# VectorE's order within an attention step: the scan in front of the low half of the turned tile

## The reference

```python
z = einsum('bqhd,bkhd->bhqk', qb, k) * (SB_HEAD_DIM ** -0.5)
log_beta = log_sigmoid(z)
log_1m = where(mask, log_beta - z, 0.0)
after = cumsum(log_1m, axis=3, reverse=True) - log_1m
a = where(mask, exp(log_beta + after), 0.0)
out = einsum('bhqk,bkhd->bqhd', a, v)
```

## Time and profile before

| what | value |
|---|---|
| median of 3 runs | 2603.29 us (2601.96 to 2605.12) |
| the profiled execution's own time | 2601.78 us |
| its span in the profile | 2600.0 us |
| granted TensorE clock, mean | 0.995 |
| TensorE busy | 2519.7 us, 97% |
| VectorE busy | 1576.0 us, 61% |
| ScalarE busy | 1152.9 us, 44% |
| POOL busy | 1169.5 us, 45% |

### The profile page before, as it was taken

One profiled execution on the slowest core, in us unless ns is written; L12 is line 12 of the kernel. 1 busy time (PEld: TensorE's weight loads), 2 busy tenths in 40 slices (PEclk: granted clock), 3 DMA queues, 4 the chain that ended last, 5 costly groups with the idle time before them and its releaser, 6 DMA issues.

```text
span 2600.0 us, 37523 instructions
## 1 busy us (share of the span) xinstructions
PE 2519.7 (97%) x13864; PEld 2149.3 (83%) x13864; DVE 1576.0 (61%) x2125; ACT 1152.9 (44%) x1932; POOL 1169.5 (45%) x1028
## 2 busy tenths in 40 slices
PE   8999899999999999999999999999999999999998
PEld 8978798787878888878788887878878887889997
DVE  3266236676435357787744477887775355867766
ACT  4366326665233135566531265656654213343333
POOL 3465435755223135456631174556653214344444
PEclk9999999999999999999999999999999999999999
DMA  6597956764446233443254244333533512233222
GB/s 229 182 277 249 343 178 190 220 207 137 136 135 244 82 114 95 132 121 112 89 188 157 97 121 119 102 110 110 148 96 114 200 65 94 75 100 110 94 95 86
DMA packets 211014, 373.91 MB, mean 144 GB/s; under 512 B 30768, under 2 KB 105136, under 8 KB 208784
## 3 DMA queue, kind: packets, MB, share of 16 engines
q1 hardware_dynamic: 210832, 371.50, 45.4%
HBM read 303.34 MB, written 68.09 MB: 143 GB/s over the span
## 4 chain that ended last, share of the span: by engine, by line
PE 83%; DVE 6%; issue 4%; DMA 2%; ACT 2%; POOL 2%; SPq 1%; POOLq 0%; ACTq 0%; DVEq 0%
PE bank L1278 27%; PE bank L1340 19%; PE bank L1228 8%; PE bank L1187 7%; PE bank L1286 7%; PE bank L1087 5%; PE bank L1134 4%; PE bank L1103 4%; DVE left L1901 1%; DMA gw_lo_raw<-in_w_in_dram 1%; POOL gw_lo L2545 1%; POOL later_lad L2571 1%; PE bank L1210 1%; DMA v_st<-v_cache_scratch 0%; DMA mixT<-mixT_scratch 0%
## 5 line engine op out<-in xcount | busy, mean ns | idle before, releaser
L1278 PE MATMUL bank<-x1T,gw_hi 128*128 128x512 f32 (+1 forms) x2336 | 712.5, 388 | 4.9 <-DVE hT_lo_raw L2002 3.5
L2475 POOL TENSOR_TENSOR beta<-beta,left 128x512 f32<-128x512 f32 (+2 forms) x326 | 350.3, 1075 | 348.6 <-DVE left L1901 347.9
L1278 PEld LDWEIGHTS bank<-x1T,gw_hi 128*128 128x128 f32 x2336 | 419.2, 189 | 84.6 <-issue 4.6
L1278 PE MATMUL bank<-x1T,gw_lo 128*128 128x512 f32 (+1 forms) x1168 | 448.1, 384 | 0.0
L2502 POOL TENSOR_TENSOR gw_lo<-gw_lo_raw,gw_hi 128x1024 fp32r<-128x1024 f32 x70 | 181.8, 2597 | 423.8 <-ACT gw_hi L1529 423.6
L1228 PE MATMUL bank<-x1T,gw_hi 128*128 128x256 f32 (+2 forms) x1472 | 356.9, 335 | 13.1 <-DVE x1T L2264 8.9
L1452 ACT ACTIVATE aT<-bank 128x512 fp32r<-128x512 f32 (+2 forms) x326 | 173.6, 533 | 424.9 <-PE bank L1103 377.3
L2177 DVE TENSOR_TENSOR acc<-bank,acc 128x512 f32<-128x512 f32 x312 | 213.7, 687 | 211.3 <-PE bank L1340 208.0
L1886 DVE TENSOR_TENSOR aT<-bank,aT 128x512 fp32r<-128x512 f32 (+2 forms) x326 | 197.2, 605 | 196.5 <-ACT aT L1452 195.2
L1340 PE MATMUL bank<-dw_hi,hT_hi 128*128 128x512 f32 x728 | 295.2, 405 | 10.8 <-issue 8.4
L1340 PE MATMUL bank<-dw_lo,hT_hi 128*128 128x512 f32 x728 | 286.7, 394 | 0.0
(11 more groups left out here) (220 smaller groups left out, 4709.2 us busy)
## 6 DMA issues: line engine op xcount, KB each, us to landing
gw_lo_raw<-in_w_gate_dram SPq DMA_DIRECT2D x88, 512.0 KB, 3.7
gw_lo_raw<-in_w_up_dram SPq DMA_DIRECT2D x88, 512.0 KB, 3.8
dw_lo_raw<-in_w_down_dram SPq DMA_DIRECT2D x86, 512.0 KB, 4.4
gw_lo_raw<-in_w_in_dram SPq DMA_DIRECT2D x64, 512.0 KB, 4.7
k_st<-kT_scratch SPq DMA_DIRECT2D x160, 128.0 KB, 4.1
v_st<-v_scratch SPq DMA_DIRECT2D x80, 256.0 KB, 4.3
q_st<-qT_scratch SPq DMA_DIRECT2D x128, 128.0 KB, 4.0
wo_raw<-in_w_out_dram SPq DMA_DIRECT2D x16, 1024.0 KB, 5.6
```

Source lines behind the costliest of these rows:

```text
L1278: m = pe.matmul(gu_bank(g, n)[:, 0:w], gw[L % 4][a][:, k, :], x1T[x][:, k, first:first + w], start=k == 0 and s == 0, stop=k == KD - 1 and ...
L2475: pool.tensor_tensor(x[:, 0:w], x[:, 0:w], left[n % RL][:, 1:w + 1], ALU.mult).then_inc(a_done, 1)
```

## The change

On VectorE, within `attention`, the block that takes the low half of the turned tile (item s - 7) moves from in front of the block that scans (item s - 1) to behind it. Waits, operands and tiles are the same, and no other engine's program is touched.

```diff
--- before.py
+++ after.py
@@ -1879,12 +1879,6 @@
                         dve.wait_ge(o_stored[og % 2], 32 * (og // 2))
                     dve.wait_ge(o_low, og + 1)
                     dve.tensor_tensor(o_t[rows, :], bank[O_BANK][0:HD, :], o_part[:, :], ALU.add).then_inc(o_sum, 1)
-                u = lo + s - AT_HI
-                if lo <= u < hi:
-                    cols = columns(u)
-                    dve.wait_ge(aT_hi, u + 1)
-                    dve.tensor_tensor(aT[u % 2][1][:, cols], bank[t_at[u]][:, cols], r32(aT[u % 2][0][:, cols]),
-                                      ALU.subtract).then_inc(aT_lo, 1)
                 n = lo + s - AT_LEFT
                 if lo <= n < hi:
                     w, out = ITEMS[n].width, left[n % RL]
@@ -1900,6 +1894,12 @@
                         added = begin[:, BW - w:BW][:, ::-1]
                     dve.tensor_tensor_scan(out[:, 0:w][:, ::-1], bank[z_at[n]][:, 0:w][:, ::-1], added, out[:, w:w + 1],
                                            ALU.mult, ALU.add).then_inc(left_done, 1)
+                u = lo + s - AT_HI
+                if lo <= u < hi:
+                    cols = columns(u)
+                    dve.wait_ge(aT_hi, u + 1)
+                    dve.tensor_tensor(aT[u % 2][1][:, cols], bank[t_at[u]][:, cols], r32(aT[u % 2][0][:, cols]),
+                                      ALU.subtract).then_inc(aT_lo, 1)
                 u = lo + s - AT_V - 2
                 if lo <= u < hi and closes_group(u) and not ITEMS[u].sample:
                     og = ITEMS[u].group
```

## The result

The changed kernel takes 2778.51 us (median, 2773.11 to 2782.61) against 2603.23 us for the kernel before: 1.0675 times as long, with a 95% interval of 1.0662 to 1.0687. The profiled execution took 2776.15 us, 174.4 us more than the one of before; its span is 2774.3 us. The forecast was 2804 us in a range of 2725 to 2868.

A forecast was written before the change was run, and what follows sets the result against it. TensorE was taken to bound the kernel. Summed turning shortfalls of 210 us, less 9 us of scan waits, plus 0, gave 201 us on 2601.78 us: 2803 us, 2804 as median; range 2725 to 2868 us.

The forecast's parts named there:

- The loop's length: Turning, copy, sigmoids, scan, low half, next turning through bank 6: at least 4.28 us, against TensorE's own 2.76 us.
- near ticks: Attention ticks one slot after the tick before: 106 of 119 predicted short, by 132 us in all.
- far ticks: Attention ticks two or more slots after the last: 133 of 177 two-slot ticks short by 78 us; the loop alone gives 43.
- so the shortfalls add: TensorE's stalls before turnings are never made up, so the ticks' shortfalls sum: 210 us, or 175 if VectorE's work gets ahead.
- the subtraction: Per tick, on the trace before: low half's new end plus hand-over, less next turning's start; positive shortfalls total 210 us.
- Waits for the scan: TensorE never again meets an unfinished scan at the scores: 9 us given back, at most 27.0.
- VectorE's tick ends later: Low half no longer fills VectorE's wait for the sigmoids, delaying work behind it: nothing taken, bound 29 us.
- TensorE's idle: Sign in the profile after: grows by some 200 us, all ahead of the last attention step.
- The slack that covers it: Rival: room between low half and next turning hides the move, within 0.2%, 2603 us; chance 0.03.
- the gain: Rival: where VectorE comes late the scan ends 0.6 us sooner; 9 to 27 us given back, 2577 to 2594 us; chance 0.02.
- The partial payment at 105 us: Rival: only short ticks cost, 132 us less 27 of waits: 2707 us, up to 2735; chance 0.11.
- The clock rival: Rival: stalls also lower TensorE's granted clock, ten to twenty drops, 27 to 54 us: 2830 to 2857 us; chance 0.06.

The follow-up runs named there:

- experiment 1: Kernel before, swap made only in ticks one slot after the previous tick: 2716.5 us; only in ticks two or more slots after: 2667.0 us.
- the one with the doubled low half: Changed kernel with the low half's subtraction done a second time into its own tile, in front of the one that counts: 2939.5 us, 161.0 above the changed kernel.

## Why the prediction was right, point by point

**What bounds, and how little the list of waits said.** Right. TensorE waited 5.6 us for the low half before, and yet moving it by 1.2 to 2.2 us cost 175 us. A wait of zero had 0.8 us behind it.

**The loop's length.** Right: forecast 4.28 us, 4.29 in the rows above. From copy to copy, the median of the 119 near ticks went from 2.85 to 4.28 us, and of the 177 ticks two slots apart from 4.05 to 4.29.

**The sum over the ticks.** The forecast was 132 us for the near and 78 us for the far ticks, and 43 for the far ones if VectorE's late work doesn't count. With the start of each next turning taken from both traces and the growth of their distance added up tick by tick, the near ticks lost 127 us and the far ones 50, together 178. (The expectations of experiment 1 count from copy to copy, which gives 105 and 73, the same total.) So the near term was right, and **the mis-sized term is the 78 us of the far ticks: 50 of them were paid.** The step that failed is "so the shortfalls add": they were read from the trace of before, one tick at a time, and a stall in a tick ahead gives the other engines time, which makes the next shortfall smaller. The far ticks fall into three groups:

| far ticks (two slots) | ticks | forecast | paid in the change | paid when only far ticks are swapped |
|---|---|---|---|---|
| VectorE late by the add of a down product | 43 | 25 us | 24 us | 25 us |
| VectorE late by other work | 22 | 18 us | 8 us | 15 us |
| VectorE's lateness adds nothing | 112 | 35 us | 19 us | 33 us |

The prediction took only VectorE's late work (35 us) for something that might shrink. But the down adds, 19 of these 35 us, wait for TensorE's own product and move with it, as in the far step shown above; they were paid. Of the 28 us that are missing, 16 are in the ticks of the third group, where the prediction saw no doubt: there ScalarE had been late. In those of them that the forecast had short, its second sigmoid came sooner behind the turning by 16 us in all, and by 2 us when only the far ticks are swapped. That the total of 50 lies so near the 43 of the lower end is luck. One tick of the third group, before:

```profile
1207.92 0.60 PE L1103 MATMUL bank<-begin,beta 128*128 128x128 f32 x4
1208.47 1.15 ACT L1496 ACTIVATE acc<-acc,rstd 128x1024 f32<-128x1024 f32 x1
...
1209.51 0.59 ACT L1452 ACTIVATE aT<-bank 128x512 fp32r<-128x512 f32 x1
...
1211.86 0.60 PE L1103 MATMUL bank<-begin,beta 128*128 128x128 f32 x4
```

After:

```profile
1283.89 1.15 ACT L1496 ACTIVATE acc<-acc,rstd 128x1024 f32<-128x1024 f32 x1
...
1285.08 0.63 PE L1103 MATMUL bank<-begin,beta 128*128 128x128 f32 x4 [1.58 <-DVE aT L1901]
...
1285.74 0.60 ACT L1452 ACTIVATE aT<-bank 128x512 fp32r<-128x512 f32 x1 [0.71 <-PE bank L1103]
...
1289.37 0.63 PE L1103 MATMUL bank<-begin,beta 128*128 128x128 f32 x4 [0.16 <-DVE aT L1901]
```

Before, a norm's scaling on ScalarE (line 1496) held the copy back to 1.59 us behind the turning, and the subtraction put the next turning 1.28 us late. After, the same scaling fell into the stall of 1.58 us ahead of the turning, the copy came after 0.66 us, and the step grew from 3.94 to 4.29 us only. With the far ticks alone swapped there is no such stall ahead: the same step took 5.21 us, 1.27 more than before.

One tick of the second group, before:

```profile
1110.20 0.38 PE L1103 MATMUL bank<-begin,beta 128*128 128x128 f32 x2
...
1111.91 0.60 ACT L1462 ACTIVATE bank<-bank 128x512 f32<-128x512 f32 x1
...
1112.36 1.59 DVE L2163 TENSOR_TENSOR hT_lo<-hT_lo_raw,hT_hi 128x512 fp32r<-128x512 f32 x1
1113.87 0.41 DVE L1886 TENSOR_TENSOR aT<-bank,aT 128x256 fp32r<-128x256 f32 x1
...
1114.52 0.27 PE L1103 MATMUL bank<-begin,beta 128*128 128x128 f32 x1
```

After:

```profile
1170.03 0.41 PE L1103 MATMUL bank<-begin,beta 128*128 128x128 f32 x2 [1.56 <-DVE aT L1901]
...
1171.61 0.68 DVE L2163 TENSOR_TENSOR hT_lo<-hT_lo_raw,hT_hi 128x512 fp32r<-128x512 f32 x1
1171.76 0.60 ACT L1462 ACTIVATE bank<-bank 128x512 f32<-128x512 f32 x1
1172.40 1.28 DVE L1895 TENSOR_TENSOR_SCAN left<-bank,left,zero_t 128x512 f32<-128x512 f32 x1
1173.60 0.40 DVE L1901 TENSOR_TENSOR aT<-bank,aT 128x256 fp32r<-128x256 f32 x1
...
1174.36 0.27 PE L1103 MATMUL bank<-begin,beta 128*128 128x128 f32 x1
```

Before, VectorE was at the hidden tile's low half until 1113.95, 2.04 us after that second sigmoid began, and the subtraction put the turning 1.09 us late. After, the same piece was done at 1172.29, ahead of the sigmoid's end, 1.51 us better: 0.60 us because it started sooner (the turning ahead had stalled for 1.56 us), and 0.91 us because it was shorter itself (see the last section). The turning came after 4.33 us, 4.32 before. Where no near tick makes such stalls, in the run that swaps only the far ticks, these ticks lost 74 us from turning to turning, near the 78 of the subtraction, while the near ticks, not swapped there, got 7 us shorter.

**Waits for the scan.** Forecast to vanish, 9 us given back. The idle ahead of the scores' matmuls went from 11.4 to 1.9 us in all; that gain is inside the 178.

**VectorE's tick ends later, taken at nothing.** In the changed kernel the 178 us between the turnings leave nothing for it in the 174 us of the whole. In the run in which only the wait was added, up to 14 us may be its share; open.

**TensorE's idle.** Forecast to grow by 200 us; the page shows 144.5 us more (80.3 to 224.8), and 29.8 us more of busy time for the same 13864 matmuls. A wide matmul is recorded with some 0.40 us while the next one starts 0.23 us after it, so the end of the last one ahead of a stall is counted as busy: 166 stalls at some 0.17 us are 28 us. The wait at line 1103 was forecast over 200 times; by its matmuls it is 166, by its weight loads 228 times.

**Rivals.** The slack that covers it and the gain fell with the result. The partial payment at 105 us fell too, since the far ticks cost 50 us in the change and 66 us by themselves; but what it names, VectorE's late work in the stalls and ScalarE running ahead, is what took 28 us off the far ticks. The clock rival has no part in the change: the granted clock was 0.99 to 1.00 in all four attention stretches of the changed kernel. It isn't empty, though; see the last section.

## What to carry to other kernels

When two pieces of work on one engine swap places, don't ask how long the queue is or how long the other engines waited for it; take a steady step from the timeline, write down the loop that closes through a single buffer (here bank 6), put into it the moved piece *and what that piece itself waits for*, and compare it with the bound engine's own work for one step. A piece whose input is released by the loop's own start must not stand in front of the loop's last step; the same piece with an early input costs little there (175 us against 20 to 42). Sum over the steps by class of distance. Where the steps ahead will stall, ask of each piece of late work, on every engine of the loop and not only on the moved one, what it waits for: a piece that waits for the bound engine moves with it and is paid in full (24 of 25 us here), and the others get out of the way in part (26 of 53 us paid).

## What the runs showed of the hardware

In the changed kernel TensorE waited for a low half 166 times, 0.97 us each in the mean and 2.5 at most, and its granted clock was 0.99 to 1.00 in all four attention stretches. With 0.6 us more in every loop it was 0.96 to 0.98. In the longest attention stretch, the changed kernel (TensorE busy for 481 of 550 us) and the one with the doubled low half (490 of 610 us, loop near 4.9 us):

```profile
1610.00:2160.00 550.00, 481.46 (x2276) 372.09 (x2275) 351.60 (x431) 273.42 (x493) 256.27 (x289) 0.99 0.33 96
```

```profile
1700.00:2310.00 610.00, 489.79 (x2208) 375.70 (x2208) 407.95 (x547) 267.31 (x485) 251.43 (x288) 0.96 0.29 85
```

A granted clock of 0.96 means that about a twelfth of the stretch ran at the lower level, 1.2 GHz. The Trainium skill (TensorE: Matmul & The Clock Gate, "Part 1: The HAM clock gate") has the array gated down to 1.2 GHz after idleness; the rows agree in direction, and with stalls of the changed kernel's size the granted clock hardly fell. In the kernel with the doubled low half a matmul that runs at half speed behind a stall may be part of the 161 us; how much of it is not separated.

The same subtraction of a hidden tile's low half on VectorE took 1.59 us in one place and 0.68 in the other (the rows above), with equal shape and operands. Beside the long one stood a product of POOL, itself at 1.99 us in place of the usual 1.09:

```profile
1111.40 1.99 POOL L2475 TENSOR_TENSOR beta<-beta,left 128x512 f32<-128x512 f32 x1 [2.71 <-DVE left L1901]
```

In the kernel before, 12 of these 84 subtractions took more than 1 us, and POOL was at work for 59 to 100% of each; for the 69 that took less than 0.7 us it was at work for 26% in the mean. So the long ones stand where POOL works beside them; no run here tests by moving one of the two whether that is the cause.
